# The memory heads of a hybrid decoder step: tokens on partitions, two heads in flight, gate rows through DRAM

## The reference

```python
def mlstm_chunk(carry, xs):
    c0, n0, m0 = carry
    q, k, v, ig, lf = xs
    cf = cumsum(lf)
    log_d = where(causal, cf[t] - cf[s] + ig[s], -inf)
    log_inter = cf + m0
    m_t = maximum(log_inter, max_s(log_d))
    w = exp(log_d - m_t) * (q @ k.T)
    s_inter = exp(log_inter - m_t)
    num = s_inter * (c0 @ q) + w @ v
    den = s_inter * (n0 @ q) + sum_s(w)
    h = num / maximum(abs(den), exp(-m_t))
    ...
    c_new = decay * c0 + sum_s wk * v * k
    n_new = decay * n0 + sum_s wk * k
    return (c_new, n_new, m_new), h

h_ml = sigmoid(om) * h
y_conv = bc * (w[0]*u[t-2] + w[1]*u[t-1] + w[2]*u[t])    # u = cc * xc
```

## Time and profile before

| | |
|---|---|
| median of 3 runs | 3279.73 us (3277.11 to 3283.16) |
| profiled execution, its own time | 3281.29 us |
| span of the trace | 3279.4 us |
| PE busy / DVE / ACT / POOL | 2967.9 / 1381.4 / 705.4 / 237.6 us |
| attention stage | about 1099 to 1198 us |
| convolution stage | 1198.0 to 1219.6 us |
| memory heads 0, 1, 2, 3 | 41.2, 44.9, 44.5, 43.9 us, to 1394.1 |
| norm, to the next phase's first product | 1394.1 to 1434.4 us |

### The profile page before, as it was taken

The page is one execution under the profiler, slowest core; times in us unless marked ns, Lnnn a source line. Parts: engine busy times, 40 slices in busy tenths (PEclk is TensorE's granted clock), DMA queues, the critical chain, the costliest instruction groups (busy, mean ns, idle before and its releaser), DMA issues. The chain is left out here.

```text
span 3279.4 us, 60260 instructions
## 1 busy us (share of the span) xinstructions
PE 2967.9 (90%) x26582; PEld 2790.9 (85%) x26582; DVE 1381.4 (42%) x1518; ACT 705.4 (22%) x913; POOL 237.6 (7%) x231
## 2 busy tenths in 40 slices
PE   5998898989999576689979999999999999999995
PEld 5997787878888355469979999999999999999995
DVE  2264445354541684452363333333333333333335
ACT  2221112122211441121152221222122112212211
POOL 0011111110100420000130000000000000000002
PEclk8999899999999786689989999999999999999997
DMA  8479999999987521024412223222222332222222
GB/s 316 131 284 390 362 355 393 362 391 369 379 336 256 163 82 48 22 62 136 137 51 86 83 89 91 90 80 89 91 82 87 91 90 82 87 91 78 90 91 81
DMA packets 332633, 547.39 MB, mean 167 GB/s; under 512 B 17545, under 2 KB 237362, under 8 KB 322578
## 3 DMA queue, kind: packets, MB, share of 16 engines
q1 hardware_dynamic: 310882, 385.00, 35.3%
q0 software_dynamic: 13872, 143.43, 10.8%
q10 hardware_dynamic: 7632, 15.20, 1.2%
HBM read 507.75 MB, written 35.83 MB: 166 GB/s over the span
## 5 line engine op out<-in xcount | busy, mean ns | idle before, releaser
L324 PE MATMUL prj_G<-prj_xh,prj_wh 128*128 128x280 f32 x1696 | 510.8, 301 | 27.9 <-DVE prj_wl L538 27.9
L326 PE MATMUL prj_G<-prj_xh,prj_wl 128*128 128x280 f32 x1696 | 503.6, 297 | 0.0
L325 PE MATMUL prj_G<-prj_xl,prj_wh 128*128 128x280 f32 x1696 | 503.4, 297 | 0.0
L545 DVE STREAM_TRANSPOSE prj_kT<-prj_k_nat 128x4096 f32<-128x4096 f32 x64 | 284.4, 4444 | 350.3 <-PE prj_S L357 350.3
L324 PEld LDWEIGHTS prj_G<-prj_xh,prj_wh 128*128 128x128 f32 x1696 | 328.9, 194 | 57.2 <-issue 30.6
L1344 PE MATMUL big_G<-big_mh,wh 128*128 128x272 f32 x1216 | 352.9, 290 | 18.7 <-issue 9.6
L1345 PE MATMUL big_G<-big_ml,big_wh 128*128 128x272 f32 x1248 | 359.5, 288 | 0.0
L1344 PE MATMUL big_G<-big_mh,big_wh 128*128 128x272 f32 x1248 | 359.2, 288 | 0.0
L1346 PE MATMUL big_G<-big_mh,big_wl 128*128 128x272 f32 x1248 | 358.2, 287 | 0.0
L1345 PE MATMUL big_G<-big_ml,wh 128*128 128x272 f32 x1216 | 351.7, 289 | 0.0
L1346 PE MATMUL big_G<-big_mh,wl 128*128 128x272 f32 x1216 | 350.9, 289 | 0.0
(11 more groups left out here) (349 smaller groups left out, 5311.5 us busy)
## 6 DMA issues: line engine op xcount, KB each, us to landing
prj_v_nat<-in_cache_v SPq DMA_DIRECT2D x256, 512.0 KB
raw<-in_w_up SPq DMA_DIRECT2D x64, 1024.0 KB, 6.4
raw<-in_w_down SPq DMA_DIRECT2D x64, 1024.0 KB, 5.0
prj_raw<-in_w_in SPq DMA_DIRECT2D x106, 512.0 KB
raw<-in_w_out SPq DMA_DIRECT2D x16, 1024.0 KB, 6.2
prj_scratch<-prj_stage ACTq DMA_DIRECT2D x53, 280.0 KB
out_xr<-x_scratch SPq DMA_DIRECT2D x16, 544.0 KB, 6.9
mix_att<-prj_scratch SPq DMA_DIRECT2D x24, 280.0 KB, 3.4
```

Of the source, the lines that this page charges most:

```text
L324: mm(out, w_hi[:, k, m], xh[:, k0 + k, cols], start=(first and k == 0), stop=False)
L325: mm(out, w_hi[:, k, m], xl[:, k0 + k, cols], start=False, stop=False)
L326: last = mm(out, w_lo[:, k, m], xh[:, k0 + k, cols], start=False, stop=(end and k == nk - 1))
L545: V.transpose(flat(kT[:, :, :, :, :].rearrange("p r h b i -> p r (h b i)")), flat(k_nat[k % 2][:, :, :]))\
```

## The change

The memory heads now keep tokens on partitions. The numerator of token tile t is a product with the weights as the stationary operand and V as the moving one, with a 129th column of ones, so that the denominator is that column. The same holds for the old state, whose 129th column is n0, with q laid out block-diagonally. Division is then by a value per partition; ScalarE does it while it copies out of PSUM, five transposes bring the head back to channels on partitions, and VectorE multiplies by the output gate. The gate rows are written to DRAM and read back, one row to all 128 partitions. Buffers `c0`, `w` and `vn` are doubled, and attention's buffers share memory with the weights. In every engine's list, the second half of head m-1 (turn back, gate, update) is laced into the first half of head m. One convolution tile is put in VectorE's list after each head's weights, before its denominators; its new state is turned once for all four tiles. SP gets the loads of `c0`, and the order of its list changes. The scalings of V move from VectorE to ScalarE.

```diff
@@ SP
             for h in range(2):
                 load_att(h)
+            for m in range(2):
+                load_mls(m)
+                load_state(m)
+            sp.wait_ge(gate_dve, 2)
+            sp.dma_start(dram["gate_scratch"][:, 0:T], fade[:, :]).then_inc(gate_out, 16)
+            sp.wait_ge(gate_act, 2)
+            sp.dma_start(dram["gate_scratch"][:, T:T + NS], enter[:, :]).then_inc(gate_out, 16)
             for c in range(2):
                 load_cnv(c)
-            for m in range(2):
-                load_mls(m)
+            sp.wait_ge(gate_out, 32)
+            for m in range(HM):
+                sp.dma_start(m_row[:, m, :], every_partition(rows[m, 0:T], T)).then_inc(rows_in, 16)
+                sp.dma_start(sbc[:, m, :], every_partition(rows[m, T:T + NS], NS)).then_inc(rows_in, 16)
             for u in range(2):
                 sp.dma_start(w_raw[:, u, :, :], dram["w_out"]...)
...
             for m in range(2, HM):
                 load_mls(m)
+                load_state(m)
@@ TensorE
+            pe.wait_ge(small_in, 16 * NSMALL)
+            for c in range(HC):
+                tr(B7[:, 128 + c * 2 * NB:...], cstate[...], ...)
+            for m in range(HM):
+                tr(B7[:, 192 + m * NB:...], n0nat[:, m, :], ...)
             pe.wait_ge(gate_act, 2)
+            for t, (t0, r) in enumerate(TT):
+                tr(B7[0:r, 64 + HM * t:...], drop[0:HM, t0:t0 + r], ...)
...
+            def gather(m):
+                if m > 0:
+                    pe.wait_ge(head_done, m)
+                pe.wait_ge(w_done, NTT * (m + 1))
+                v = vn[m % 2]
+                for t, (t0, r) in enumerate(TT):
+                    if t < 4:
+                        for k in range(t + 1):
+                            mm(N[t], ws[k][:, t0 - k0:t0 - k0 + P], v[:, k, :], ...)
+                    else:
+                        mm(N[4][0:TAIL, :], ws[4][0:TAIL, :], v[0:TAIL, 4, :], ...)
+                        for k in range(4):
+                            mm(N[4][0:NMETA, :], ws[k][...], v[:, k, :], ...)
+                pe.wait_ge(qsc_done, m + 1)
+                pe.wait_ge(c0_copied, m + 1)
+                for b in range(NB):
+                    last = mm(N[4][0:TAIL, :], qsc[:, b, :], c0T[:, b, :], ...)
+                last.then_inc(num_ps, 1)
+            for m in range(HM + 1):
+                if m < HM:
+                    begin(m)
+                if m > 0:
+                    turn_head(m - 1)
+                if m < HM:
+                    similar(m, 0)
+                    similar(m, 4).then_inc(sml_ps, 1)
+                if m > 0:
+                    update(m - 1)
+                if m < HM:
+                    turn_state(m)
+                    similar(m, 1).then_inc(sml_ps, 1)
+                    ...
+                    gather(m)
@@ ScalarE, per head
...
+                for k in range(NTT):
+                    A(vwp[0:kr, k, :], v[0:kr, k, 0:HD], ACT.Copy, scale=wm[k][0:kr, last_col:last_col + 1])
+                for b in range(NB):
+                    ins = A(vws[:, b, :], v[0:TAIL, 4, 0:HD], ACT.Copy, scale=wm[4][0:TAIL, col:col + 1])
+                ins.then_inc(vw_done, 1)
+                ac.wait_ge(den_done, m + 1)
+                for t, (t0, r) in enumerate(TT):
+                    ins = A(hn[0:r, t, :], N[t][0:r, 0:HD], ACT.Copy, scale=inv[0:r, t:t + 1])
+                ins.then_inc(hn_done, 1)
+            ac.wait_ge(cnew_ps, 1)
+            A(cout[:, :], B4[0:2 + 2 * NB, :], ACT.Copy).then_inc(cout_done, 1)
             ac.wait_ge(w_in, 32)
             A(wh0[:, :, :], w_raw[:, 0, :, :], ACT.Copy).then_inc(w_hi0, 1)
@@ VectorE
+            dv.wait_ge(rows_in, 32 * HM)
+            for m in range(HM + 1):
+                if m < HM:
+                    arguments(m)
+                if m > 0:
+                    gate_head(m - 1)
+                if m < HM:
+                    weights(m, 0)
+                    weights(m, 1)
+                if m > 0:
+                    update(m - 1)
+                if m < HM:
+                    weights(m, 2)
+                    weights(m, 3)
+                    weights(m, 4)
+                    old_state(m)
+                    convolve(m)
+                    denominators(m)
@@ GpSimd
-            step(G_.memset(rows[:, :], 0.0))
...
-            step(G_.memset(onehot3[:, :], 0.0))
-            for base in (0, 32, 64):
-                step(select(onehot3[:, :], ALU.not_equal, -base, [[-1, HM]], 1.0))
...
-                if m < HM - 1:
-                    po.dma_start(c0[:, :, :], dram["state_C"][0, :, m + 1]...)
```

More of the change, by code:

```diff
@@ L616, in phase_mix @@
         kvn = [sb(f"kvn{i}", [P, 2, NTT, HD]) for i in range(2)]
[L617 to L620, removed]
+        shared = sb("shared", [P, 6 * T + 1 + 8 * P])
+        prob = [shared[:, i * T:(i + 1) * T] for i in range(2)]
+        kept, left = shared[:, 2 * T:3 * T], shared[:, 3 * T:4 * T + 1]
+        attn = [shared[:, (4 + i) * T + 1:(5 + i) * T + 1] for i in range(2)]
+        attnT = [shared[:, 6 * T + 1 + 4 * P * i:6 * T + 1 + 4 * P * (i + 1)].rearrange("p (k n) -> p k n", k=4) for i in range(2)]
         attnT4 = sb("attnT4", [P, NTT, TAIL])
@@ new lines, in begin, with similar @@
+                if m > 0:
+                    pe.wait_ge(c0_copied, m)
+                natural(v_T, k_T, KV[0], KV[1], B6)
+            def similar(m, k):
+                q_T, k_T, v_T, o_T = mls[m % 2]
+                k0, kr = TT[k]
+                if k == 0:
+                    mm(SCORE[0], k_T[:, 0:P], q_T[:, 0:512], start=True, stop=True)
+                    return mm(B5[:, 0:NMETA], k_T[:, 0:P], q_T[:, 512:TP], start=True, stop=True)
+                end = T if k == 4 else TP
+                return mm(SCORE[k][0:kr, :], k_T[:, k0:k0 + kr], q_T[:, k0:end], start=True, stop=True)
@@ L884, in mlstm_head, with turn_head, update @@
                 last.then_inc(num_ps, 1)
-                pe.wait_ge(vwp_done, m + 1)
+            def turn_head(m):
+                pe.wait_ge(hn_done, m + 1)
+                for t, (t0, r) in enumerate(TT):
+                    last = tr(H4 if t == 4 else B7[:, t0:t0 + r], hn[0:r, t, :], ident[0:r, 0:r])
+                last.then_inc(h_ps, 1)
+            def update(m):
+                k_nat, wm = kn[m % 2], w[m % 2]
+                pe.wait_ge(vw_done, m + 1)
+                pe.wait_ge(h_done, m + 1)
@@ L907, in _ @@
+            pe.wait_ge(conv_done, HC)
+            for c in range(HC):
+                last = tr(B4[0:2 + 2 * NB, c * P:(c + 1) * P], cnew[:, c, :], ident[:, :])
+            last.then_inc(cnew_ps, 1)
             pe.wait_ge(norm_consts, 5)
@@ L1222, in mlstm_head, with gate_head, update @@
+            def gate_head(m):
+                o_T = mls[m % 2][3]
+                dv.wait_ge(h_ps, m + 1)
+                V.tensor_tensor(hT[:, HA + HC + m, 0:512], B7[:, :], o_T[:, 0:512], ALU.mult)
+                V.tensor_tensor(hT[:, HA + HC + m, 512:T], H4, o_T[:, 512:T], ALU.mult).then_inc(h_done, 1)
+            def update(m):
                 dv.wait_ge(cp_ps, m + 1)
-                for b in range(NB):
-                    ins = V.tensor_scalar(vw[0:TAIL, b, :], nat[0:TAIL, 0, 4, :], ecol[0:TAIL, 4, 1 + b:2 + b], None, ALU.mult)
@@ L1232, in mlstm_head @@
                 dv.wait_ge(cs_ps, m + 1)
+                state = c0[m % 2]
                 for b in range(NB):
                     last = NQ * b + NQ - 1
-                    ins = V.scalar_tensor_tensor(c0[:, b, :], c0[:, b, :], sbc[:, last:last + 1],
+                    ins = V.scalar_tensor_tensor(state[:, b, :], state[:, b, :], sbc[:, m, last:last + 1],
                                                  G[0][:, b // 4, b % 4 * P:(b % 4 + 1) * P], ALU.mult, ALU.add)
                 ins.then_inc(head_done, 1)
-            for m in range(HM):
-                mlstm_head(m)
+            dv.wait_ge(rows_in, 32 * HM)
```

378 lines of the change are left out of this document (167 added, 211 removed).

## The result

| | before | after |
|---|---|---|
| median, same chip | 3281.44 us (3277.11 to 3290.65) | 3191.11 us (3184.14 to 3195.69) |
| ratio, 95% interval | | 0.9719 [0.9691, 0.9748] |
| span of the profiled execution | 3279.4 us | 3193.9 us |
| end of attention to the first norm product (the stage) | 196.1 us | 102.6 us |

The forecast was 3200 us, faster at 0.97. It is faster, by 90 us where 80 were forecast. The stage is measured from VectorE's first instruction on `uext` (1209.27 in the trace of after) to the first norm product (1311.90).

A forecast was written before the change was run, and what follows sets the result against it. In the mixing phase's memory heads no engine was the bound; each waited for another in turn. Head 0, heads 1 to 3 and the tail put the norm 82.7 us earlier, 79.7 after hops: 3201.6 profiled, forecast 3200 us, range 3187 to 3230.

The forecast's parts named there:

- Head 0: First memory head after attention: TensorE free at 1200.1, numerators from 1209.5, lasting 7.5 us and ended at 1217.
- Heads 1 to 3: The three later memory heads: 24 us each, with 5 more before head 2, 77 in all, to 1294.
- Which clock: TensorE's clock in the new heads: 0.86 by busy share between attention and the old heads, giving 24.1 us a head.
- The stall: TensorE waiting for memory head 2's late tiles, queued behind convolution tile 3's: 5 us (0 at 1.2 GHz, 7 at 2.4).
- The tail: From head 3's numerators to the first norm matmul: output, update at the mixed clock, w_out's split, squares; 17.5 us.
- Hops: Some 30 engine-to-engine hops in the stage, each 0.1 us more than counted: 3 us added.
- all at 2.4 GHz: Fast bound of the stage: 21.3 us a head, first norm matmul at 1302.6, -91.6 us, total 3188 us.
- The clock stays low: Rival: TensorE stays at its lower clock in the memory heads; time 3235 us, chance 0.12.
- waits (a) and (b): TensorE's waits per head: before the output transposes (2.0 us fast, 0.7 slow) and before the numerators (1.7 fast, 0.7 slow).
- Loads come late: Rival: the in-order SP queue delays attention head 2's tiles or memory head 2's or 3's; 3220 us, chance 0.12.
- The heads do not overlap: Rival: ScalarE or VectorE order makes heads wait for each other, convolution uncovered; 30 us a head, 3225 us, chance 0.05.
- Slower, by slow broadcasts: Rival: reading one DRAM row for 128 partitions delays attention; for instance 3290 us at 27 us each, chance 0.02.

## Why the prediction was right, and where its terms were off

The direction, the place and the mechanism hold: the gain lies in the stage, and attention is as it was (132.7 us from the phase's start before, 130.4 to 133.4 in the nine kernels above whose front is the same as that of after). The trace of after has 135.0. No engine waited for a load there; TensorE ran some 6 us of attention's front at 1.2 GHz. The sum had -79.7 us for the stage; it measured 196.1 - 102.6 = 93.5. The profiled spans differ by 85.5: in this trace the phase started 8.8 us later, attention took 2.4 more, and what follows the stage 3.2 less. The medians differ by 90.3. Term by term:

- **Head 0**: forecast 18.9 us from the end of attention to the end of its numerators, measured 16.0: -2.9. Part of this is luck of the trace, since seven of the nine kernels took 17.5 to 18.0.
- **Heads 1 to 3**: forecast 24 + 29 + 24 = 77, measured 67.2: -9.8. This is the term of the sum that was mis-sized, and the step that failed in it is *Which clock*: 0.86, drawn between attention and the old heads by the busy share. The windows show 1.00 in undisturbed heads, and the run with one head after the other shows that the busy share does not order the clock: 83% busy stood at 0.70 there and at 1.00 when laced. At 1.00 the prediction's own lengths give 21.3 us; the measured 20.1 are 16.7 us busy and waits of 1.4 and 2.0. Numerators took 5.6 us (1266.60 to 1272.24) and not 6.4; the 3.4 us of waits were forecast as 3.7.
- **The stall** before head 2: forecast 5 between 0 and 7, measured 6.9 in the period. At the full clock it is the upper bound, as the prediction's own bounds say; it is inside the 67.2.
- **The tail**: forecast 17.5, measured 19.5: +2.0. Here the clock went the other way: 0.60 where the mixed one was assumed, so that the update's products stretched over 9.2 us and not 7.2.
- **Hops**: 3 us added, none seen: -3.0.

Together -2.9 - 9.8 + 2.0 - 3.0 = -13.7, and -79.7 - 13.7 = -93.4. The stage came out 1.9 us beyond the bound "all at 2.4 GHz" (-91.6). That bound had 17.9 us for head 0, 70.9 for heads 1 to 3 with the stall and 15.7 for the tail, against 16.0, 67.2 and 19.5, so the slow tail took back 3.8 of the 5.6 us by which the heads came in under that bound. Two slips in the working change nothing: the mean of the two clocks is 24.0 us a head and not 24.1, and the tail's items add up to 17.3 and not 17.5.

What was costed at nothing: the convolution inside the heads (right, 1.38 us spare where 1.7 were forecast, period unchanged without it); ScalarE's scalings (right, 4.0 us against 4.0, and they matter where they stand: on VectorE they cost 10.3 us of stage); SP's queue (right, but with 2.4 us to spare and not 8); the front of the phase (no change that the spread of the traces would show).

The rivals. *The clock stays low*: in the nine laced kernels (the one after and eight of the experiments), 23 of 27 periods were at 1.00, and none stood at 1.2 GHz throughout; heads run one by one sat at 0.70 to 0.93. The rule of the Trainium skill (TensorE: Matmul & The Clock Gate, Part 1) that activity releases a throttled default, which the step on the clock named, is borne out in so far as filled gaps raised the clock. The condition that the prediction added, that waits (a) and (b) might count as idle every time, was not met: 1.4 and 2.0 us in every head left it at 1.00. The reading that the old heads had the lowest clock overlooked the convolution stage, where TensorE waited more and had 0.58. *Loads come late*: one did, as forecast in the sum, 7 us; attention's did not, but with eight more row reads ahead of them they came 5.8 us late. *The heads do not overlap*: they do, at 20.1 us. *Slower, by slow broadcasts*: the eight row reads were issued within 7.3 us, and those of 560 values landed a median of 9.5 us after their issue.

## What to carry to other kernels

Take a stage's two prices, at 1.2 and at 2.4 GHz, from rows, and ask which waits remain between the products: lacing two items was worth its gaps and, more, the clock that came with them (1.6 to 2.5 us of gaps, 4.2 to 8.7 in all). Don't interpolate the clock between stages by their busy share; give the two prices as bounds. Read the last item of a laced loop by itself, for it has nothing to lace with: here the tail ran at 0.60, and two small moves of work into it gave 13.3 us. When an instruction is moved ahead to shorten a wait, look at whether it was the cover of that same wait. In an in-order queue of loads, list what each load waits for, and put those that wait longest last.

## What the runs showed of the hardware

The clock falls and recovers in ways that the length of one wait does not settle. With the scalings on VectorE a 2.50 us wait lowered it, and TensorE then worked without a gap for 15 us at 1.2 GHz before it rose; the same wait one head later, 2.51 us, did not. The 1.95 us wait before the numerators left it at 1.00 in two heads of the run with all convolutions ahead, and lowered it in the third. After the 7.19 us stall it was back sooner, in the kernel after:

```profile
1250.50:1253.10 2.60, 0.62 (x3) 0.63 (x4) 0.00 (x0) 0.00 (x0) 0.00 (x0) 0.50 0.96 316
1253.10:1255.70 2.60, 2.60 (x15) 2.27 (x13) 0.00 (x0) 0.79 (x3) 0.00 (x0) 0.58 0.04 12
1255.70:1258.30 2.60, 2.60 (x16) 1.92 (x16) 2.09 (x7) 2.22 (x7) 0.00 (x0) 1.00 0.21 45
```

Some 3 us of work, then 1.00. And head 0, with the same waits of 1.3 and 1.4 us ahead of its numerators, lost 1.5 to 2.0 us to the low clock in seven kernels and nothing in two. What decides between these stays open; the traces show only that with fewer and shorter waits the low stretches were rarer (23 of 27 laced periods at 1.00, none of the six with one head after the other). The other surprise is the load of a 280 KB tile right behind 2 MB of another stream: 7.1 and 7.8 us to landing for the first one, where the median of its kind is 3.4.
